# A decoder step on one Trainium2 core: the third sub-layer's conditioning moved from the opening stage into the first FFN

## The chip, the core and the metric

One core of a Trainium2 chip runs the whole kernel. TensorE (PE; its weight loads are listed as PEld), VectorE (DVE), ScalarE (ACT), GpSimd (POOL) and SyncE (SP, which here only issues transfers) each work through a queue of their own and wait for one another by semaphores. The metric is the time of one execution on the device, in microseconds (us).

## The reference

A decoder of two layers, each a token mixer and a SwiGLU feed-forward block (FFN), so four sub-layers. All activations are held transposed, 1024 features by 1056 tokens (1024 of the prompt, 32 of eight sampled sequences). Each sub-layer is conditioned: shift, scale and gate come from a product of the nine conditioning vectors with a 1024 x 3072 matrix.

```python
def modulation(c, w, b):
    m = jax.nn.silu(c) @ w + b
    shift, scale, gate = jnp.split(m, 3, axis=-1)
    return shift[:, None, :], scale[:, None, :], gate[:, None, :]

for i in range(DEPTH):
    sh, sc, gt = modulation(c, ada_w[i, 0], ada_b[i, 0])
    h = rmsnorm(x, norm_g[i, 0]) * (1 + sc) + sh
    ...                                   # layer 0: pooling mixer, layer 1: sparse attention
    x = x + gt * out
    sh, sc, gt = modulation(c, ada_w[i, 1], ada_b[i, 1])
    h = rmsnorm(x, norm_g[i, 1]) * (1 + sc) + sh
    x = x + gt * swiglu(h, ffn_w_in[i], ffn_w_out[i])
```

## The kernel before

Phases follow one another, with a barrier between them: `front_phase` (the opening stage: conditioning of sub-layers 1 to 3 and the pooling mixer), `ffn_phase` for layer 0, attention, `ffn_phase` for layer 1, the final norm.

**Conditioning.** The matrix of a sub-layer comes in six quads of 2 MB (QN = 6). For a quad, PE multiplies: 32 matmuls (64 records in the trace, since each fp32 matmul is recorded twice) whose stationary tile is 128 x 32, the nine vectors padded to 32, and which write four 32-row strips of bank 6 of PSUM (`multiply`, L337). ACT copies the sums to SBUF (L344), and PE turns them with one matmul into bank 7 (L352, two records). When all six quads are turned, DVE adds the bias and scales (L202, L205). `d.ada` lies in HBM as 24 quads, four sub-layers of six.

**Opening stage.** SP loads x and then the 18 quads of sub-layers 1 to 3 into a ring of three buffers (L437). After the first six quads come four pooling groups: DVE makes differences, ACT scales two tiles of the group (L459), PE multiplies them (L528), DVE adds the result to x (L562). The other twelve quads stand in PE's and ACT's queues between the groups, by the list `between`: quads 6 and 7 after group 0, 8 to 10 after group 1, 11 and 12 after group 2, 13 to 17 after group 3. After group 3 come also the products of the sampled tokens (L536) and their residual on DVE (L569, L570). The last steps of DVE are the conditioning of sub-layer 3.

**FFN.** It begins with an RMS norm: ACT squares (L247), PE sums over features (L255), DVE makes variance and reciprocal (L275, L280). The hidden size of 2816 is cut into N = 11 iterations. An iteration has three weight units of 1 MB: two hidden tiles of the up projection (each with a gate and an up side) and one unit of the down projection. Each fp32 unit is split into a high and a low part: ACT writes the high one (L677), POOL the rest (L718), and every product is three matmuls (L748 to L750, L768 to L770). Iteration 0 stands by itself; iterations 1 to 10 are a loop on each engine. In an iteration PE makes six groups of gate and up products (two tiles by three column chunks of 352 tokens; one group is 48 matmuls) and then, for each column chunk, eight down products (48 matmuls). SP loads the next iteration's units: unit 0 into `raw` 0 and unit 1 into `raw` 1 when POOL has split unit 2 of the current iteration, and unit 2 into `raw` 0 when it has split the next unit 0 (L662). Banks 0 to 5 of PSUM are in use; banks 6 and 7 are free after the norm.

The fourth sub-layer's conditioning is made during the attention's input stage, in half quads between fp32 matmuls (L369).

Of the kernel before, what the change touches and what calls it, by code (L numbers as in the profile page):

```python
# [14 lines left out]
ACT = mybir.ActivationFunctionType  # L15
# [8 lines left out]
P = 128  # L24
# [355 lines left out]
def front_phase(nc, c, d):  # L380
# [3 lines left out]
    with ExitStack() as ctx:  # L384
# [29 lines left out]
        block = ctx.enter_context(nc.Block())  # L414
        mod = QuadModulation(c, mrow, lambda n: ada[:, n % RING, :], lambda pe, n: pe.wait_ge(ada_ready[n % RING], 16 * (n // RING + 1)),
                             used, row_ready, turned, sums_read)
        NQ = (SUBS - 1) * QN

        between = [range(6, 8), range(8, 11), range(11, 13), range(13, NQ)]

        def cols(ch):
            return slice(ch * CH, (ch + 1) * CH)
# [118 lines left out]
        def _(dve):  # L541
# [77 lines left out]
            modulation(1)  # L619
            residuals(3)  # L620
            sample_residuals()
            modulation(2)
            dve.wait_ge(added, 24)


def ffn_phase(nc, c, d, layer):
# [3 lines left out]
    with ExitStack() as ctx:  # L630
# [12 lines left out]
        silu_ready, gated, a_step, a_ready = sem("silu_ready"), sem("gated"), sem("a_step"), sem("a_ready")  # L643
        added, rstep = sem("added"), sem("rstep")
        src = d.ffn[layer]
        block = ctx.enter_context(nc.Block())

        FIRST = [(a, ch) for ch in range(NCH) for a in range(2)]
# [2 lines left out]
        @block.sync  # L651
        def _(sp):

            sp.dma_start(raw[:, 0, :], src[0]).then_inc(raw_ready[0], 16)
            sp.dma_start(raw[:, 1, :], src[1]).then_inc(raw_ready[1], 16)
            sp.wait_ge(w_lo, 1)
            sp.dma_start(raw[:, 0, :], src[2]).then_inc(raw_ready[0], 16)
            with sp.Fori(0, N - 1) as i:
                for a in range(3):

                    sp.wait_ge(w_lo, i * 3 + (3, 2, 4)[a])
                    sp.dma_start(raw[:, a % 2, :], src[bass.ds(i * 3 + 3 + a, 1)].rearrange("a p n -> (a p) n")).then_inc(raw_ready[a % 2], 16)  # L662

        def raw_count(a, i):
            return (i * 16 + 16) if a == 1 else (i * 32 + (16 if a == 0 else 32))

        @block.scalar
        def _(act):
            def split_hi(a, i, first=False):
                act.wait_ge(raw_ready[a % 2], raw_count(a, i))  # L670
                if not first:

                    if a < 2:
                        act.wait_ge(up_ready, i * 6 - (3 if a == 0 else 0))
                    else:
                        act.wait_ge(down_ready, i * GD)
# [12 lines left out]
            norm.act_std(act, 1)  # L689
            split_hi(0, 0, True)  # L690
            norm.act_squares(act, 18, 24)
            norm.act_hi(act, 0, 8)
            split_hi(1, 0, True)
            norm.act_hi(act, 8, 14)
            silus(0, 1, 0)
            norm.act_hi(act, 14, 16)
            split_hi(2, 0, True)
            silus(1, 2, 0)
            norm.act_std(act, 2)
            norm.act_sample_hi(act)  # L700
            norm.act_hi(act, 16, 24)
            silus(2, 6, 0)
            act.wait_ge(up_ready, 6)
            for a in range(3):
                split_hi(a, 1)
            with act.Fori(1, N - 1) as i:
                silus(0, 3, i)
                split_hi(0, i + 1)
                silus(3, 6, i)
                split_hi(1, i + 1)  # L710
                split_hi(2, i + 1)
            silus(0, 6, N - 1)

        @block.gpsimd
# [12 lines left out]
        def _(pe):  # L727
            for ch in range(NCH):
                norm.pe_sums(pe, ch)

            def iteration(i, first):
                for n, (a, ch) in enumerate(FIRST if first else LATER):
                    pe.wait_ge(w_lo, 3 * i + (a + 1))
                    hi = whi[:, a, :].rearrange("p (k s m) -> p k s m", k=KD, s=2)
                    lo = wlo[:, a, :].rearrange("p (k s m) -> p k s m", k=KD, s=2)
                    col = slice(ch * CH, (ch + 1) * CH)
                    for side in range(2):
                        bank = 2 * (n % 3) + side
                        if n < 3 and not first:
                            pe.wait_ge(added, i * GD + (bank - 5))  # L740
                        if n >= 3:
                            pe.wait_ge(gated if side else silu_ready, i * 6 + (n - 2))
                        for k in range(KD):
                            if first and a == 0 and side == 0:
                                pe.wait_ge(norm.lo_ready, KD * ch + k + 1)
                                if ch == 2 and k == 0:
                                    pe.wait_ge(norm.s_lo, 1)
                            pe.matmul(c.ps[:, bank, 0:CH], hi[:, k, side, :], hhi[:, k, col], start=(k == 0), stop=False)  # L748
                            pe.matmul(c.ps[:, bank, 0:CH], lo[:, k, side, :], hhi[:, k, col], start=False, stop=False)  # L749
                            last = pe.matmul(c.ps[:, bank, 0:CH], hi[:, k, side, :], hlo[:, k, col], start=False, stop=(k == KD - 1))  # L750
                        last.then_inc(up_ready if side else gate_ready, 1)
                pe.wait_ge(w_lo, 3 * i + 3)
                hi = whi[:, 2, :].rearrange("p (k m) -> p k m", k=2)
                lo = wlo[:, 2, :].rearrange("p (k m) -> p k m", k=2)
                for ch in range(NCH):
                    col = slice(ch * CH, (ch + 1) * CH)
                    pe.wait_ge(a_ready, i * 6 + (2 * ch + 2 if first else NCH + ch + 1))
                    for m in range(KD):
                        q = ch * KD + m
                        if q < 6 and q % 2 == 0:  # L760
                            pe.wait_ge(silu_ready, i * 6 + (NCH + q // 2 + 1))
                        if q < 6 and q % 2 == 1:
                            pe.wait_ge(gated, i * 6 + (NCH + q // 2 + 1))
                        if q >= 6:
                            pe.wait_ge(added, i * GD + (q - 5))
                        w = slice(m * P, (m + 1) * P)
                        for k in range(2):
                            pe.matmul(c.ps[:, q % 6, 0:CH], hi[:, k, w], ahi[:, k, col], start=(k == 0), stop=False)  # L768
                            pe.matmul(c.ps[:, q % 6, 0:CH], lo[:, k, w], ahi[:, k, col], start=False, stop=False)  # L769
                            last = pe.matmul(c.ps[:, q % 6, 0:CH], hi[:, k, w], alo[:, k, col], start=False, stop=(k == 1))  # L770
                        last.then_inc(down_ready, 1)
            iteration(0, True)
            with pe.Fori(1, N) as i:
                iteration(i, False)

        @block.vector
        def _(dve):
# [49 lines left out]
            with dve.Fori(1, N) as i:  # L827
                for n, (a, ch) in enumerate(LATER):
                    gating(n, a, ch, i)
                residuals(i)  # L830
            dve.wait_ge(added, N * GD)


# [1381 lines left out]
```

## Time and profile before

| | |
|---|---|
| time, three runs | 2593.82, 2596.44, 2597.05 us; median 2596.44 |
| profiled execution | 2593.58 us, its span 2592.0 us |
| busy: PE, PEld | 2394.1 us (92%), 2061.1 us (80%) |
| busy: DVE, ACT, POOL | 1150.0, 670.6, 590.2 us |
| opening stage | 0 to 137 us |
| first FFN | 137 to 917 us |
| mean granted clock of PE | 0.969 of full speed |

The span is what the profiler saw of the execution on the core; the time contains it and 1.6 us around it. Busy time of an engine counts its instructions without register, branch, semaphore and transfer-issuing ones. A row of the timeline gives the start, the time to the end of the last of its merged instructions, engine, line, operation, tiles written and read with their shapes, the number of instructions, and in brackets the idle time of the engine before it and what ended it.

### The profile page before, as it was taken

The page shows a single profiled execution, that of the slowest core. Times are in us where ns is not written, and L with a number is a line of the kernel's source. Part 1 is how long each engine was busy: PE and PEld are TensorE (multiplying, and loading weights), DVE is VectorE, ACT ScalarE, POOL GpSimd, SP SyncE. Part 2 cuts the span into 40 slices and gives each one's busy share as a digit, 9 for nine tenths or more (in the row PEclk, how much of TensorE's full clock was granted, in tenths as well). Part 3 has the DMA queues.
Part 4 walks back from the last instruction along what each step waited for, and adds up shares of the span by engine and source line. Part 5 has one row for each costly group of instructions (what it writes and reads, how often), then busy time and mean ns, then how long its engine had stood idle before and what let it go on. Part 6 is the DMA issues. An engine that isn't in the chain of part 4 may idle for free. (4 is left out here: it accounts for less than half of the span.)

```text
span 2592.0 us, 39643 instructions
## 1 busy us (share of the span) xinstructions
PE 2394.1 (92%) x14980; PEld 2061.1 (80%) x14980; DVE 1150.0 (44%) x2604; ACT 670.6 (26%) x1193; POOL 590.2 (23%) x428
## 2 busy tenths in 40 slices
PE   4889999999999998899879976598999999999997
PEld 3679999999999964376535433397999999999995
DVE  7574333333333342787467631324633333333336
ACT  2151111111111042677167641204211111111101
POOL 2203112222122014200056643210221222221211
PEclk8999999999999999999989997799999999999998
DMA  9712111100111033243120019501101111111101
GB/s 403 296 51 82 49 49 49 49 29 36 49 49 49 0 139 106 85 144 115 56 84 17 9 55 308 210 18 50 61 38 49 49 49 49 49 49 49 49 0 67
DMA packets 67700, 206.59 MB, mean 80 GB/s; under 512 B 9589, under 2 KB 31637, under 8 KB 55061
## 3 DMA queue, kind: packets, MB, share of 16 engines
q1 hardware_dynamic: 54256, 179.01, 18.9%
q0 software_dynamic: 7920, 21.22, 2.5%
q10 hardware_dynamic: 5428, 5.12, 0.7%
q8 instruction: 57, 0.93, 0.1%
q14 instruction: 39, 0.31, 0.0%
HBM read 188.52 MB, written 16.13 MB: 79 GB/s over the span
## 5 line engine op out<-in xcount | busy, mean ns | idle before, releaser
L748 PE MATMUL ps<-f_hhi,f_whi 128*128 128x352 f32 x2112 | 682.6, 323 | 4.0 <-DVE f_hlo L295 3.6
L749 PE MATMUL ps<-f_hhi,f_wlo 128*128 128x352 f32 x2112 | 676.8, 320 | 0.0
L750 PE MATMUL ps<-f_hlo,f_whi 128*128 128x352 f32 x2112 | 676.5, 320 | 0.0
L718 POOL TENSOR_TENSOR f_wlo<-f_raw,f_whi 128x2048 fp32r<-128x2048 f32 x62 | 285.3, 4603 | 1224.7 <-ACT f_whi L677 1041.1
L80 DVE SCALAR_TENSOR_TENSOR xT<-ps,mod,xT 128x352 f32<-128x352 f32 (+1 forms) x552 | 313.9, 572 | 206.7 <-PE ps L770 121.6
L748 PEld LDWEIGHTS ps<-f_hhi,f_whi 128*128 128x128 f32 x2112 | 396.1, 188 | 8.2 <-DVE f_hlo L295 6.4
L749 PEld LDWEIGHTS ps<-f_hhi,f_wlo 128*128 128x128 f32 x2112 | 396.8, 188 | 0.0
L750 PEld LDWEIGHTS ps<-f_hlo,f_whi 128*128 128x128 f32 x2112 | 396.0, 188 | 0.0
L768 PE MATMUL ps<-f_ahi,f_whi 128*128 128x352 f32 x1056 | 340.6, 323 | 0.0
L769 PE MATMUL ps<-f_ahi,f_wlo 128*128 128x352 f32 x1056 | 338.4, 320 | 0.0
L770 PE MATMUL ps<-f_alo,f_whi 128*128 128x352 f32 x1056 | 338.2, 320 | 0.0
L677 ACT ACTIVATE f_whi<-f_raw 128x2048 fp32r<-128x2048 f32 x66 | 126.2, 1916 | 543.3 <-PE ps L770 414.9
L783 DVE TENSOR_TENSOR f1n_g<-f1n_sq,ps 128x352 f32<-128x352 f32 x66 | 34.4, 521 | 383.4 <-PE ps L750 382.7
L783 DVE TENSOR_TENSOR f0n_g<-f0n_sq,ps 128x352 f32<-128x352 f32 x66 | 34.4, 521 | 383.4 <-PE ps L750 382.6
L769 PEld LDWEIGHTS ps<-f_ahi,f_wlo 128*128 128x128 f32 x1056 | 198.4, 188 | 0.0
L768 PEld LDWEIGHTS ps<-f_ahi,f_whi 128*128 128x128 f32 x1056 | 198.1, 188 | 0.0
L770 PEld LDWEIGHTS ps<-f_alo,f_whi 128*128 128x128 f32 x1056 | 198.0, 187 | 0.0
L1647 POOL TENSOR_TENSOR pa_pr<-pa_pr,pa_rl 128x128 f32<-128x128 f32 (+7 forms) x128 | 143.9, 1146 | 162.3 <-DVE pa_rl L1635 162.2
L1086 PE MATMUL ps<-oT,ai_w 128*128 128x352 f32 x480 | 149.4, 466 | 0.0
L1625 DVE CUSTOM_DVE_ANT_0 pa_pr<-ps,mb 128x128 f32<-128x128 f32 (+7 forms) x128 | 91.9, 755 | 97.2 <-PE ps L1559 96.8
L1086 PEld LDWEIGHTS ps<-oT,ai_w 128*128 128x128 f32 x480 | 89.8, 191 | 48.3 <-issue 3.3
L684 ACT ACTIVATE f0n_sq<-ps 128x352 f32<-128x352 f32 x66 | 30.6, 465 | 340.2 <-PE ps L750 340.2
(311 smaller groups left out, 2832.7 us busy)
## 6 DMA issues: line engine op xcount, KB each, us to landing
f_raw<-in_ffn SPq DMA_DIRECT2D x66, 1024.0 KB, 4.8
ada_raw<-in_ada SPq DMA_DIRECT2D x18, 2048.0 KB, 12.3
sa_kv<-in_ckv POOLq DMA_DIRECT2D x54, 256.0 KB, 4.6
xT<-in_ada SPq DMA_DIRECT2D x12, 1024.0 KB, 5.4
sa_kv<-in_ckv SPq DMA_DIRECT2D x42, 256.0 KB, 4.7
ai_w<-in_win SPq DMA_DIRECT2D x6, 1024.0 KB, 7.1
xT<-in_ckv SPq DMA_DIRECT2D x23, 256.0 KB, 2.7
xT<-in_xT SPq DMA_DIRECT2D x8, 528.0 KB, 7.7
```

The lines of the kernel that those rows point to most:

```text
L80: ins = dve.scalar_tensor_tensor(out=x, in0=psum[:, 0:n], scalar=gate[:, 0:1], in1=x, op0=ALU.mult, op1=ALU.add)
L677: act.activation(whi[:, a, :], raw[:, a % 2, :], ACT.Copy).then_inc(w_hi, 1)
L718: pool.tensor_tensor(wlo[:, a, :], raw[:, a % 2, :], whi[:, a, :].bitcast(F32), ALU.subtract).then_inc(w_lo, 1)
L748: pe.matmul(c.ps[:, bank, 0:CH], hi[:, k, side, :], hhi[:, k, col], start=(k == 0), stop=False)
L749: pe.matmul(c.ps[:, bank, 0:CH], lo[:, k, side, :], hhi[:, k, col], start=False, stop=False)
L750: last = pe.matmul(c.ps[:, bank, 0:CH], hi[:, k, side, :], hlo[:, k, col], start=False, stop=(k == KD - 1))
L768: pe.matmul(c.ps[:, q % 6, 0:CH], hi[:, k, w], ahi[:, k, col], start=(k == 0), stop=False)
L769: pe.matmul(c.ps[:, q % 6, 0:CH], lo[:, k, w], ahi[:, k, col], start=False, stop=False)
L770: last = pe.matmul(c.ps[:, q % 6, 0:CH], hi[:, k, w], alo[:, k, col], start=False, stop=(k == 1))
L1086: ins = pe.matmul(c.ps[:, n % 4, 0:CH], wt[:, k, job[1] * P:(job[1] + 1) * P], h[:, k, cols(job[2])], start=(k == 0), stop=(k == KD - 1))
L1625: dve.tensor_tensor_reduce(out=probs(i, 2 * sp + a, 0, L), in0=src, in1=c.mb[:, MB0[q]:MB0[q] + L], scale=-SCALE, scalar=-NEG, op0=ALU.add ...
L1647: pool.tensor_tensor(p, p, rl[:, s // 2 % 4, r:r + 1].to_broadcast([P, (pairs[i][0] + 1) * P]), ALU.mult).then_inc(p_ready, 1)
```

## The change

The opening stage makes twelve quads instead of 18: 6 and 7 after group 0, 8 and 9 after group 1, 10 and 11 after group 2, none after group 3; the third sub-layer's two DVE steps go with it. In the first FFN each of iterations 1 to 6 makes one quad of the third sub-layer, in four parts of 16 matmul records on PE: after the second and the sixth up group and after the first and second chunk of the down products. After the third chunk PE turns the quad. The weights come in quarter quads of 512 KB, in pieces of 1 KB, into the norm's `rstd` buffer, which is free by then; a part's load waits until the part before is used. ACT copies the sums between the splits of units 1 and 2. DVE makes the two steps of the conditioning after the last residual of the FFN. The FFN's loops on SP, ACT and PE are cut in two: iterations 1 to 6 with the new work, 7 to 10 without. The second FFN gets none.

```diff
-        NQ = (SUBS - 1) * QN
-        between = [range(6, 8), range(8, 11), range(11, 13), range(13, NQ)]
+        NQ = 2 * QN
+        between = [range(6, 8), range(8, 10), range(10, NQ), []]
...
             sample_residuals()
-            modulation(2)
...
+        PARTS = 4
+        COND = QN if layer == 0 else 0
+        ada = norm.rstd[:, 0:2 * UNIT // PARTS].rearrange("p (j k m) -> p j k m", j=4, k=KD // PARTS)
...
+                with sp.Fori(1, COND + 1) as i:
+                    load(i, (0, 1))
+                    for part in range(PARTS):
+                        if part == 1:
+                            load(i, (2,))
+                        sp.wait_ge(mod_used, i * PARTS + (part + 1 - PARTS))
+                        quad = d.ada[bass.ds(i + (2 * QN - 1), 1)].rearrange("a p (j k m) -> (a p) j k m", j=4, k=KD)
+                        sp.dma_start(ada, quad[:, :, KD // PARTS * part:KD // PARTS * (part + 1), :]).then_inc(ada_ready, 16)
...
                 split_hi(1, i + 1)
+                if conditioning:
+                    act.wait_ge(mod_used, i * PARTS + 1)
+                    act.wait_ge(turned, i)
+                    act.activation(mrow[:, :], c.ps[:, 6, 0:P], ACT.Copy).then_inc(row_ready, 1)
                 split_hi(2, i + 1)
...
+            def condition(i, part):
+                pe.wait_ge(ada_ready, i * (16 * PARTS) + 16 * (part + 1 - PARTS))
+                if part == 0:
+                    pe.wait_ge(row_ready, i)
+                for k in range(KD // PARTS):
+                    for j in range(4):
+                        last = pe.matmul(c.ps[32 * j:32 * j + 32, 6, 0:P], c.silu[:, KD // PARTS * part + k, :], ada[:, j, k, :],
+                                         start=(part == 0 and k == 0), stop=(part == PARTS - 1 and k == KD // PARTS - 1))
+                last.then_inc(mod_used, 1)
+            def turn(i):
+                pe.wait_ge(row_ready, i + 1)
...
+                pe.matmul(out, mrow[:, :], pick, start=True, stop=True).then_inc(turned, 1)
...
+                    if conditioning and n in (1, 5):
+                        condition(i, n // 5)
...
+                    if conditioning and ch < 2:
+                        condition(i, 2 + ch)
+                    if conditioning and ch == 2:
+                        turn(i)
...
                 residuals(i)
+            if COND:
...
+                Modulation(c, None, None, None, None, None, turned, sums_read).apply(dve, 2, QN + 1, 0, link)
             dve.wait_ge(added, N * GD)
```

## Rows read from the trace of the kernel before

**Rows 1.** The page, part 1: span and busy time of PE and its weight loads.

```profile
span 2592.0 us, 39643 instructions
PE 2394.1 (92%) x14980; PEld 2061.1 (80%) x14980; DVE 1150.0 (44%) x2604; ACT 670.6 (26%) x1193; POOL 590.2 (23%) x428
```

**Rows 2.** By stretches: length, busy us (instructions) per engine, granted clock, DMA share, GB/s.

```profile
65.00:130.00 65.00, 52.88 (x834) 40.16 (x832) 36.55 (x56) 9.27 (x17) 13.32 (x15) 0.97 0.78 295
260.00:325.00 65.00, 65.00 (x411) 65.00 (x410) 24.23 (x58) 8.11 (x9) 11.07 (x3) 1.00 0.13 49
```

**Rows 3.** Timeline, end of the opening stage and start of the FFN.

```profile
116.31 1.95 PE L337 MATMUL ps<-ada_raw,silu 128*32 128x128 f32 x64
116.88 0.42 DVE L570 TENSOR_TENSOR xT<-xT,pool_tmp 128x256 f32<-128x256 f32 x1
119.00 1.95 PE L337 MATMUL ps<-ada_raw,silu 128*32 128x128 f32 x64
136.11 0.38 DVE L202 TENSOR_TENSOR mod<-ps,vec 128x216 f32<-128x216 f32 x1 [18.80 <-PE ps L352]
136.52 0.23 DVE L205 SCALAR_TENSOR_TENSOR mod<-mod,vec 128x72 f32<-128x72 f32 x1
137.28 2.04 ACT L247 ACTIVATE f0n_sq<-xT 128x352 f32<-128x352 f32 x5 [1.74 <-PEq L384]
```

**Rows 4.** Timeline, from quad 10 to the pooling group behind it.

```profile
89.31 2.18 ACT L459 ACTIVATE pool_df<-pool_df,mod 128x1024 f32<-128x1024 f32 x2
91.54 7.15 PE L528 MATMUL ps<-pool_df,pool_raw 128*128 128x352 f32 x24 [1.66 <-ACT pool_df L459]
```

**Rows 5.** The FFN's start: two stretches (as rows 2), then two rows of the timeline.

```profile
140.00:142.00 2.00, 2.00 (x5) 1.23 (x4) 0.00 (x0) 0.65 (x3) 0.00 (x0) 0.50 1.00 414
152.00:154.00 2.00, 0.81 (x3) 0.59 (x4) 1.97 (x2) 2.00 (x5) 0.00 (x0) 1.00 0.00 0
...
137.82 7.88 PE L255 MATMUL ps<-f0n_sq,ones 128*128 128x352 f32 x20 [1.82 <-ACT f0n_sq L247]
144.56 0.52 DVE L275 TENSOR_SCALAR f0n_rstd<-ps 128x352 f32<-128x352 f32 x1 [7.80 <-PE ps L255]
```

**Rows 6.** Timeline of PE, attention's input stage: half quads between wide fp32 matmuls.

```profile
979.81 27.38 PE L1069 MATMUL ps<-oT,ai_w 128*128 128x352 f32 x92
...
1089.80 0.28 PE L1128 MATMUL ps<-ai_part,rowsum 128*128 128x1 f32 x2
1090.00 1.08 PE L369 MATMUL ps<-xT,silu 128*32 128x128 f32 x32
1091.01 3.23 PE L1086 MATMUL ps<-oT,ai_w 128*128 128x352 f32 x10
1094.08 0.28 PE L1128 MATMUL ps<-ai_part,rowsum 128*128 128x1 f32 x2
1094.22 0.39 PE L352 MATMUL ps<-ident,ai_mrow 128*128 128x36 f32 x2
1094.54 1.08 PE L369 MATMUL ps<-xT,silu 128*32 128x128 f32 x32
```

**Rows 7.** Page, part 5 (mean ns); L337 alone (ns min/median/max); timeline at a switch of width.

```profile
L770 PE MATMUL ps<-f_alo,f_whi 128*128 128x352 f32 x1056 | 338.2, 320 | 0.0
...
L337 PE MATMUL ps<-ada_raw,silu x1152: 272/273/423, 22.1 to 134.8; 128*32 128x128 f32 x192
...
98.62 1.69 PEld L337 LDWEIGHTS ps<-ada_raw,silu 128*32 128x32 f32 x64 [0.44 <-issue]
```

**Rows 8.** An FFN iteration's weight units: timeline, one stretch, loads (us to landing).

```profile
298.26 1.92 ACT L677 ACTIVATE f_whi<-f_raw 128x2048 fp32r<-128x2048 f32 x1 [20.91 <-PE ps L770]
305.03 0.92 SPq L662 DMA_DIRECT2D f_raw<-in_ffn  x2
...
311.00:312.00 1.00, 1.00 (x8) 1.00 (x7) 0.00 (x0) 0.00 (x0) 0.00 (x0) 1.00 0.57 238
...
f_raw<-in_ffn SPq DMA_DIRECT2D x66, 1024.0 KB, 4.8
```

More of the change, by code:

```diff
@@ L645, in ffn_phase @@
         src = d.ffn[layer]
+        PARTS = 4
+        COND = QN if layer == 0 else 0
+        ada = norm.rstd[:, 0:2 * UNIT // PARTS].rearrange("p (j k m) -> p j k m", j=4, k=KD // PARTS)
+        mrow = sb("mrow", [P, P]) if COND else None
+        ada_ready, mod_used, row_ready, turned, sums_read, m_step = [sem(n) for n in ("ada_ready", "mod_used", "row_ready", "turned", "sums_read", "m_step")]
         block = ctx.enter_context(nc.Block())
@@ L657, in _, with load @@
             sp.dma_start(raw[:, 0, :], src[2]).then_inc(raw_ready[0], 16)
-            with sp.Fori(0, N - 1) as i:
-                for a in range(3):
+            def load(i, units):
+                for a in units:
                     sp.wait_ge(w_lo, i * 3 + (3, 2, 4)[a])
                     sp.dma_start(raw[:, a % 2, :], src[bass.ds(i * 3 + 3 + a, 1)].rearrange("a p n -> (a p) n")).then_inc(raw_ready[a % 2], 16)
+            with sp.Fori(0, 1) as i:
+                load(i, (0, 1, 2))
+            if COND:
+                sp.wait_ge(norm.lo_ready, KD * NCH)
+                sp.wait_ge(norm.s_lo, 1)
+                with sp.Fori(1, COND + 1) as i:
[6 more added lines that the diff above has]
+                        sp.dma_start(ada, quad[:, :, KD // PARTS * part:KD // PARTS * (part + 1), :]).then_inc(ada_ready, 16)
+            with sp.Fori(COND + 1, N - 1) as i:
+                load(i, (0, 1, 2))
         def raw_count(a, i):
@@ L705, in _, with body @@
                 split_hi(a, 1)
-            with act.Fori(1, N - 1) as i:
+            def body(i, conditioning):
                 silus(0, 3, i)
@@ L710, in _ @@
                 split_hi(1, i + 1)
+                if conditioning:
+                    act.wait_ge(mod_used, i * PARTS + 1)
+                    act.wait_ge(turned, i)
+                    act.activation(mrow[:, :], c.ps[:, 6, 0:P], ACT.Copy).then_inc(row_ready, 1)
                 split_hi(2, i + 1)
+            if COND:
+                with act.Fori(1, COND + 1) as i:
+                    body(i, True)
+            with act.Fori(COND + 1, N - 1) as i:
+                body(i, False)
             silus(0, 6, N - 1)
@@ L729, in _, with iteration @@
                 norm.pe_sums(pe, ch)
-            def iteration(i, first):
+            def condition(i, part):
[9 more added lines that the diff above has]
+                pe.wait_ge(row_ready, i + 1)
+                pick = c.ident[:, :].rearrange("p (j e) -> p j e", j=4)[:, :, 0:NSQ]
+                out = c.ps[:, 7, bass.ds(i * (4 * NSQ) - 4 * NSQ, 4 * NSQ)].rearrange("p (j e) -> p j e", j=4)
+                pe.matmul(out, mrow[:, :], pick, start=True, stop=True).then_inc(turned, 1)
+            def iteration(i, first, conditioning=False):
                 for n, (a, ch) in enumerate(FIRST if first else LATER):
@@ L771, in iteration @@
                         last.then_inc(down_ready, 1)
+                    if conditioning and ch < 2:
+                        condition(i, 2 + ch)
+                    if conditioning and ch == 2:
+                        turn(i)
             iteration(0, True)
-            with pe.Fori(1, N) as i:
+            if COND:
+                for counter in (mod_used, row_ready, turned):
+                    pe.sem_inc(counter, 1)
+                with pe.Fori(1, COND + 1) as i:
+                    iteration(i, False, True)
+            with pe.Fori(COND + 1, N) as i:
                 iteration(i, False)
@@ L830, in _, with link @@
                 residuals(i)
+            if COND:
+                steps = [0]
+                def link(ins):
+                    steps[0] += 1
+                    ins.then_inc(m_step, 1)
+                    dve.wait_ge(m_step, steps[0])
+                Modulation(c, None, None, None, None, None, turned, sums_read).apply(dve, 2, QN + 1, 0, link)
             dve.wait_ge(added, N * GD)
```

## The prediction

> **What bounds the kernel now.** I read the page's busy shares first: TensorE (PE) works 92% of the span [rows 1]. That is a mean over stages, so the table by stretches comes next, and it shows two stages of different kind. In the first feed-forward block (FFN) PE and its weight loads are busy without a gap: 411 matmuls in 65.00 us, one each 0.158 us, at the full granted clock, while no other engine fills half its time [rows 2]. Whatever PE is given there lengthens the kernel by its full duration. In the opening stage (65 to 130 us) PE works 53 of 65 us [rows 2]; there the order of the work decides, and the timeline shows it. Third view: what PE does last in the opening stage. From the sample residuals (VectorE, DVE, done at 116.88 + 0.42 = 117.30 us) to the first square of the FFN (ScalarE, ACT, 137.28 us) nothing happens but the last five quads of the third sub-layer's conditioning and its two DVE steps [rows 3]. So the change takes work from a place where it alone is on the path and puts it where PE is full. The question is only the price in each.
>
> **What is removed.** (a) Five quads and the conditioning's two DVE steps after the fourth pooling group: from 117.30 to 136.52 + 0.23 = 136.75 us, 19.45 us [rows 3]. (b) One quad fewer ahead of the fourth group: quad 10 now follows group 2 and quad 12 is gone. A quad costs 119.00 - 116.31 = 2.69 us there, because product, ACT copy and turn follow one another [rows 3]. It is on the path: ACT scales the next group's tiles (89.31 us) only behind the copy of the last quad's sums, which stands ahead in its queue, and PE's pooling matmuls wait for that scaling (91.54) [rows 4]. Sum: 22.1 us. Late next would be the DVE residuals; they follow the same PE chain and move with it. The weight queue on SP is empty then, so the FFN's first loads start as soon as before. No piece of it stays: bound from 19.5 (b gains nothing) to 22.1; I take 22.1, since the chain in rows 4 is complete.
>
> (c) The clock at the FFN's start. Before, PE came from the last quads, short bursts between waits for weights and copies, and between 140 and 142 us it had 0.50 of its clock, so the first twenty records of the sums took 7.88 us [rows 5]. Between 152 and 154 us, after a wait that followed solid work, it kept 1.00 [rows 5]. With the change PE comes from solid pooling matmuls and a wait of about 2 us. The first chunk's sixteen records then take 16 x 0.296 = 4.7 us (27.38 us for 92 such records [rows 6]); with 0.3 for the last one's end the variance on DVE could start at 137.82 + 5.0 = 142.8 instead of 144.56 [rows 5]: 1.7 us, on the path, since square root and every later tile follow it. Bounds 0 and 1.7; I take 1.7, the case nearest to the row at 152.
>
> **What is added on PE.** In each of iterations 1 to 6: 64 narrow matmul records (32 output columns) in four parts of 16, and one turn of two records. Nothing hides them. Streaming: 64 records take 1.95 us, the last one's own 0.27 apart, so 0.0267 us each; a part streams 0.43 us. But each part stands among wide matmuls. The trace has this for the fourth sub-layer, half a quad between fp32 matmuls of the attention input [rows 6]: 32 records occupy 1091.01 - 1090.00 = 1.01 us where streaming gives 0.85 (0.16 on leaving); the ten wide records behind them need 1094.08 - 1091.01 = 3.07 where ten of 0.296 are 2.96 (0.11, a weight load not hidden); entering costs 0.20 (1089.80 to 1090.00) against 0.14 where no narrow block follows (1094.08 to 1094.22), 0.06. So 0.33 us for each insertion, whatever its size, and a part costs 0.43 + 0.33 = 0.76. The turn takes 1094.54 - 1094.22 = 0.32, with the entry into a narrow block; 0.26 without. Per iteration 4 x 0.76 + 0.26 = 3.30 us, six times: 19.8 us. Splitting a quad in four thus costs more PE time (3.3) than the serial quad did in the opening stage (2.69). Bounds of a part: 0.43, if the neighbours cover the switch, and 0.98, if the whole pause of 0.44 us in the weight loads that stands at such a switch in the opening stage [rows 7] comes on top of the streaming and of the 0.11 behind it. I take 0.76, from the row with the same narrow tiles between dense wide ones.
>
> [...]
>
> What a full drain would do, from rows: a wide FFN record lasts 0.32 and follows at 0.158, so entering costs 0.16; a narrow one lasts 0.27 and follows at 0.107 for four, so leaving costs 0.17; with the 0.11 a part costs 0.87, the six iterations 22.4 us [rows 2, 7].
>
> **What is added elsewhere.** ACT: one copy an iteration, which waits for the fourth part. Queued behind it is the split of the third unit, and that waits for the end of the down products anyway, 7.6 us (48 x 0.158) later. PE's turn waits for that copy with the same 7.6 us in hand. Cost 0. DVE: the two steps (0.38 + 0.23, 0.65 with the gap [rows 3]) now follow the FFN's last residual, and the phase ends with them: +0.7.
>
> SP: four loads of 0.5 MB an iteration. Parts 1 to 3 have time: a part's buffer is free when the part before is used, 7.6 us or more ahead of its use, and a load twice as big lands in 4.8 us [rows 8]. The load of unit 2 is queued behind part 0 only, which waits for nothing. **Part 0 is tight.** Its load is queued on SP behind units 0 and 1 of the next iteration, which start when GpSimd has split unit 2: 298.26 (end of the down products) to 305.03 [rows 8]. Their data flow until the slice 311 to 312, 57% of it [rows 8]; half a megabyte more at that rate ends near 312.9, with 1 KB pieces and the receipt 313.4 to 313.8. PE wants it after two column blocks, 96 x 0.158 = 15.2 us after 298.26, plus the turn: 313.5 to 313.7. So PE waits 0 to 0.4 us in each iteration; I take 0.2, 1.2 us in all. Bounds 0 and 6 (1 us in each).
>
> **The sum.** -22.1 - 1.7 + 19.8 + 1.2 + 0.7 = -2.1 us. The profiled execution took 2593.58 us (span 2592.0), 2.9 under the median of the three runs, 2596.44; the sum is made in its rows and applied to the median: 2594.3 us.
>
> **Rivals.**
> 1. *The switches are covered.* FFN matmuls take half the time of the fp32 ones in rows 6, so what surrounds a part is not the same; if they hide the switch, a part costs near 0.43, six iterations 11.9, and the kernel gains 10.0: 2586. From 0.63 a part it is faster by over 5.2 us. For it: PE's gaps at group ends in the FFN are nil [rows 2]. Against it: rows 6.
> 2. *Part 0 comes late* (the other side). PE is stopped behind a wait in every conditioning iteration, by the queue of 2 MB ahead of it. If it lands 1.4 us after PE wants it, 8.4 us instead of 1.2, and with the clock's 1.7 not won: +6.8, 2603. It decides from some 1.2 us per iteration on. For it: there is no margin in the rows 8. Against it: the data rate leaves 0.4 at most.
> 3. *Full drain*, as priced above: +0.5, 2597, which no measurement here tells from the forecast.
> 4. *The opening stage doesn't shorten as said*, because another end takes over (the pooling tail's output, GpSimd's wait for it): half the gain lost would give +9, 2605. That output follows DVE's tail step, which moves earlier too, so little speaks for it.
>
> **How the numbers follow.** Forecast 0.42, full drain 0.15, covered switches 0.25, late part 0 0.15, opening not shortened 0.03. About 0.2%, 5.2 us, can be told from no change; forecast and drain lie inside: same 0.57, faster 0.25, slower 0.18. The range takes a part at 0.58 with no wait (-22.1 - 1.7 + 15.5 + 0.7 = -7.6) and a part at 0.9 with the clock not won and 0.4 us of waiting (-22.1 + 23.2 + 2.4 + 0.7 = +4.2): 2588.8 to 2600.6, widened to 2588.5 and 2601.5 for a piece of rival 2. The far ends of rivals 1 and 2 stay out.
>
> **What the changed profile would show.** The FFN's first square near 115 us instead of 137.28; sums matmuls at clock 1.00 behind it; iterations 1 to 6 of 68.7 + 3.3 + 0.2 us, 7 to 10 unchanged at 68.7 (432 x 0.159); at a part, 16 narrow records within 0.43 and the next wide record about 0.3 later than streaming alone; no PE idle released by the weight load at parts 1 to 3, some tenths at part 0; the DVE steps 0.7 us behind the last residual. A wait of a microsecond at part 0, an iteration under 71.2 or over 73.4 us, or an FFN start later than 118 us would make the forecast wrong.

## The result, and the profile after

The changed kernel takes 2597.79 us (median of 20 runs, 2593.14 to 2602.45); the kernel before, in the runs beside it, 2593.51. The ratio is 1.0017 with a 95% interval of 1.0010 to 1.0024: 4.4 us more, between 2.6 and 6.2. The forecast was 2.1 us less. The profiled execution of the changed kernel took 2601.43 us. Its page, part 1, against [rows 1]:

```profile
span 2599.8 us, 39755 instructions
PE 2406.2 (93%) x14980; PEld 2064.0 (79%) x14980; DVE 1151.0 (44%) x2604; ACT 671.1 (26%) x1193; POOL 591.3 (23%) x428
```

PE has the same number of matmul records and is busy 12 us longer. The end of the opening stage, against [rows 3] and [rows 4] (timeline: start, length, engine, line, operation):

```profile
102.02 2.17 ACT L459 ACTIVATE pool_df<-pool_df,mod 128x1024 f32<-128x1024 f32 x2
...
104.25 8.85 PE L528 MATMUL ps<-pool_df,pool_raw 128*128 128x352 f32 x24 [1.66 <-ACT pool_df L459]
112.93 4.19 PE L536 MATMUL ps<-pool_fs,pool_raw 128*128 128x32 f32 x32
...
117.61 0.42 DVE L570 TENSOR_TENSOR xT<-xT,pool_tmp 128x256 f32<-128x256 f32 x1
118.55 1.65 ACT L247 ACTIVATE f0n_sq<-xT 128x352 f32<-128x352 f32 x4 [14.36 <-PEq L384]
```

The first square follows the sample residual after 0.94 us and not after 20.40. It stands at 118.55 and not near 115: pooling group 3, at half clock from 105.6 to 109.0, took 8.85 us where group 2 took 7.15 [rows 4], the products of the samples took 4.19 us and not 3.65, and DVE's first conditioning step came 1.6 us later than in the first profile of the kernel before. (Half clock is a granted clock of 0.50.) The next view is the table by stretches (length, busy us (instructions) of PE, PEld, DVE, ACT, POOL, granted clock, DMA share, GB/s), against [rows 2] and [rows 5]: the opening stage, the first sums, iterations 1, 3 and 7.

```profile
65.00:130.00 65.00, 55.30 (x543) 39.08 (x542) 41.14 (x61) 15.92 (x30) 14.82 (x16) 0.92 0.36 134
119.00:122.00 3.00, 2.90 (x5) 1.85 (x6) 0.00 (x0) 1.85 (x6) 0.00 (x0) 0.50 0.83 268
211.10:284.89 73.79, 72.05 (x500) 70.31 (x499) 24.47 (x59) 8.82 (x10) 13.81 (x3) 1.00 0.21 72
357.39:429.41 72.02, 72.02 (x502) 70.36 (x500) 24.37 (x59) 8.82 (x10) 13.82 (x3) 1.00 0.21 73
646.39:715.13 68.74, 68.74 (x436) 68.74 (x434) 24.10 (x58) 8.55 (x9) 13.83 (x3) 1.00 0.13 47
```

The first sums run at half clock again. Iteration 3 takes 3.3 us more than iteration 7; iteration 1 takes 73.79 us, with PE idle for 1.7 of them. The timeline of a part of 16 records, with the wide matmuls around it (against [rows 6]), and of the turn:

```profile
259.33 0.32 PE L801 MATMUL ps<-f_hlo,f_whi 128*128 128x352 f32 x1
259.59 0.64 PE L772 MATMUL ps<-f0n_rstd,silu 128*32 128x128 f32 x16
260.16 0.43 PE L821 MATMUL ps<-f_ahi,f_whi 128*128 128x352 f32 x1
260.43 0.32 PE L822 MATMUL ps<-f_ahi,f_wlo 128*128 128x352 f32 x1
...
429.11 0.32 PE L823 MATMUL ps<-f_alo,f_whi 128*128 128x352 f32 x1
429.27 0.30 PE L780 MATMUL ps<-ident,f_mrow 128*128 128x36 f32 x2
429.41 0.41 PE L799 MATMUL ps<-f_hhi,f_whi 128*128 128x352 f32 x1
429.65 0.32 PE L800 MATMUL ps<-f_hhi,f_wlo 128*128 128x352 f32 x1
```

From 259.33 to 260.43 there are 1.10 us; without the part there would be two spacings of 0.159, so the part costs 0.78. The turn: 429.65 - 429.11 - 2 x 0.159 = 0.22. The last lines are for part 0 of iteration 1, against [rows 8]: SP's issues, and PE's wait for the load.

```profile
218.14 0.98 SPq L669 DMA_DIRECT2D f_raw<-in_ffn  x2
219.41 0.70 SPq L683 DMA_DIRECT2D f0n_rstd<-in_ada  x1
...
226.24 0.32 PE L801 MATMUL ps<-f_hlo,f_whi 128*128 128x352 f32 x1
228.30 0.64 PE L772 MATMUL ps<-f0n_rstd,silu 128*32 128x128 f32 x16 [1.74 <-DMA f0n_rstd<-in_ada]
```

One profile of each kernel doesn't settle a difference of 4 us, since the stretches at half clock lie elsewhere from profile to profile (pooling group 3 takes 8.85 us in the first of the changed kernel and 7.15 in the second). So both were profiled again (experiment 6), and the stages, read from the timelines, stand beside the terms of the prediction (us):

| stage | before (3 profiles) | changed (2 profiles) | predicted | measured |
|---|---|---|---|---|
| start to DVE's first conditioning step | 53.84, 55.51, 55.30 | 55.41, 55.27 | 0 | +0.5 |
| to the last sample residual (L570) | 63.04, 63.01, 62.77 | 62.20, 60.19 | -2.7 | -1.7 |
| to the FFN's first square | 20.40, 20.56, 20.54 | 0.94, 0.95 | -19.45 | -19.6 |
| to the first up matmul | 19.53, 19.53, 19.53 | 19.60, 20.81 | -1.7 | +0.7 |
| iteration 0 | 72.60, 72.94, 72.45 | 72.94, 72.45 | 0 | 0 |
| iterations 1 to 6 | 411.96, 412.01, 411.96 | 435.29, 434.63 | +21.0 | +23.0 |
| to the attention's first square | 277.28, 277.30, 277.30 | 278.04, 278.06 | +0.7 | +0.8 |
| sum | | | -2.1 | +3.6 |

The sum by stages, 3.6, lies in the runs' interval of 2.6 to 6.2. It is not the whole difference between these profiles: their spans are 2592.0, 2590.6 and 2589.9 us before and 2599.8 and 2600.0 after, 9.1 apart in the mean, so 5.5 us lie behind the attention's first square, where the code is the same. That stretch takes 1667.2 to 1673.3 us in the seven profiles of this case without quads in the FFN and 1672.8 to 1678.7 in the seven with them. The runs leave room for at most some 3 us of it; whether any of it is an effect of the change stays open.

### The profile page after: what moved, and what is told of

It is laid out like the page before. It is cut to its first block and busy times, and to the rows that moved or that the text cites. A ratio compares the mean times of both kernels' runs of the same rounds, so it can differ in the third digit from the quotient of the medians.

```text
span 2599.8 us, 39755 instructions
## 1 busy us (share of the span) xinstructions
PE 2406.2 (93%) x14980; PEld 2064.0 (79%) x14980; DVE 1151.0 (44%) x2604; ACT 671.1 (26%) x1193; POOL 591.3 (23%) x428
## 3 DMA queue, kind: packets, MB, share of 16 engines
q1 hardware_dynamic: 66064, 179.01, 19.2%
```

## The experiments

**1. Only the removal.** The third sub-layer's conditioning isn't made at all.

```diff
-        COND = QN if layer == 0 else 0
+        COND = 0
...
             modulation(1)
+            link(dve.tensor_copy(c.mod[:, 2], c.mod[:, 1]))
```

> Only the removal: the opening without the third sub-layer's six quads, and nothing in the FFN in their place. The third sub-layer's conditioning is left out of the computation (it takes the second's vectors, one copy on VectorE), so the time is that of the cheaper opening alone. Theory A, the prediction's term: the opening gives 22.1 us, and the total is 21 to 23 us under the kernel before (about 2571.5 beside 2593.5). Theory A with the clock term of the prediction: 23.8 us under. Theory B, read from the one profile of the changed kernel, whose first square came 18.7 us earlier: the opening gives 18 to 19 us, because the stretches at half clock in the opening last as long as before.

Measured: ratio to the kernel before 0.9912 (0.9895 to 0.9929), 22.8 us less, between 18.4 and 27.2. The middle lies between theory A's 22.1 and its 23.8 with the clock term; the interval excludes neither, and of theory B's 18 to 19 only the lower end.

**2. Only the addition.** All eighteen quads stay in the opening stage (`NQ` and `between` as before, `modulation(2)` kept), and the FFN makes six of them again.

> Only the addition: the opening as before, with all eighteen quads and the third sub-layer's conditioning made there, and the six quads made a second time in iterations 1 to 6 of the first FFN, as in the change. The prediction's terms: 19.8 us on TensorE, 1.2 us for the weights of part 0 and 0.7 us on VectorE, so 21.7 us over the kernel before. Theory A, with the sizes in the profile of the changed kernel: 20.1 us for parts and turns, 2.4 us for part 0's waits, 0.8 us by which the matmuls behind part 0 follow each other more slowly, 0.7 us on VectorE: 24 us over. Theory B, that the addition costs as predicted and the opening gave less: 21 to 22 us over.

Measured: 1.0106 (1.0083 to 1.0129), 27.5 us more, between 21.5 and 33.5. The total holds both theories, but the two halves add up to +4.7, near the change's own +4.4, so no further mechanism is needed; with the intervals of both halves this sum is known to some 7 us only. In its profile iterations 1 to 6 take 436.24 us, 24.3 more than before, and part 0 of iteration 1 waits again, 2.0 us. Some 1.5 of the 24.3 are a stretch at half clock right behind that wait (253.6 to 257.0 us); in the two profiles of the changed kernel no such stretch follows it.

**3. Part 0's load ahead of the units.**

```diff
                 with sp.Fori(1, COND + 1) as i:
-                    load(i, (0, 1))
                     for part in range(PARTS):
                         if part == 1:
-                            load(i, (2,))
+                            load(i, (0, 1, 2))
```

> The changed kernel with one line of SyncE moved: part 0 is asked for ahead of units 0 and 1 of the iteration, and no longer behind the wait for unit 1's buffer. If TensorE's waits for the quarter quad at part 0 (2.1 us and 0.4 us in the profile of the changed kernel) come from the place of that issue in the queue, the total falls by 2.0 to 2.8 us against the changed kernel (about 2595.3 beside 2597.8). If they come from the free buffer, or from how long the transfer takes, it falls by under 0.5 us; if unit 0 or 1 comes late in its stead, it rises.

Measured: 1.0004 (0.9995 to 1.0013) where the changed kernel has 1.0017, 3.4 us less by the ratios, and by their intervals between 0.4 and 6.3. Its profile (issues on SP, PE at part 0, stretches of iterations 1 and 2, and the times from issue to landing of the 24 loads, least, median, most; the last line is the changed kernel's):

```profile
206.75 0.70 SPq L682 DMA_DIRECT2D f0n_rstd<-in_ada  x1
216.39 0.97 SPq L669 DMA_DIRECT2D f_raw<-in_ffn  x2
...
224.69 0.64 PE L771 MATMUL ps<-f0n_rstd,silu 128*32 128x128 f32 x16
...
209.34:281.29 71.95, 71.95 (x501) 70.29 (x499) 24.53 (x60) 8.83 (x10) 13.82 (x3) 1.00 0.23 78
281.29:353.31 72.02, 72.02 (x502) 70.36 (x500) 24.41 (x59) 8.82 (x10) 13.82 (x3) 1.00 0.21 73
...
DMA to landing us min/median/max: 3.6/3.7/6.0
```

```profile
DMA to landing us min/median/max: 3.6/4.9/8.8
```

The load is issued 18 us ahead of its use and not 7, PE has no idle time in the two iterations, and units 0 and 1 aren't late. Iterations 1 to 6 take 432.07 us: the queue ahead of part 0 cost 3.2 and 2.6 us in the two profiles of the changed kernel, and 20.1 us are left for parts and turns. Some 0.8 of the 3.2 was not a wait: behind part 0 of iterations 2 and 6 the wide matmuls followed at 0.161 us where 0.159 is usual. Here, and in the second profile of the changed kernel, it is absent or half as large; its cause stays open.

**4. Two insertions instead of four.** The same 64 records an iteration, in two blocks of 32 behind the sixth up group and the second down chunk; the second quarter's weights lie in free parts of other buffers.

```diff
-                    if conditioning and n in (1, 5):
-                        condition(i, n // 5)
+                    if conditioning and n == 5:
+                        condition(i, 0)
...
-                    if conditioning and ch < 2:
-                        condition(i, 2 + ch)
+                    if conditioning and ch == 1:
+                        condition(i, 1)
```

> The changed kernel with the same matmuls in two insertions of 32 for an iteration and not in four of 16, behind the sixth up group and the second down group, with a second buffer for the weights. Theory A, an insertion has a price of its own, about 0.35 us beside the time of its matmuls: 12 insertions fewer give 4.2 us; the first insertion no longer waits for its weights (2.4 us), and the up groups behind the second one keep the spacing that they had (0.8 us): 6 to 7.5 us under the changed kernel, near 2591 beside 2597.8, which is 2 to 3 us under the kernel before. Theory B, the price goes with the matmuls and not with the insertions: only the waits are saved, 2 to 3 us under the changed kernel. Theory C, longer insertions let VectorE or the weight units fall behind: no gain.

Measured: 0.9998 (0.9990 to 1.0007), 4.9 us under the changed kernel (by the intervals 2.1 to 7.8), level with the kernel before. Iterations 1 and 2 in its profile, and a block of 32:

```profile
208.26:279.49 71.23, 71.23 (x501) 70.40 (x499) 24.54 (x60) 8.82 (x10) 13.81 (x3) 1.00 0.22 75
279.49:350.79 71.30, 71.30 (x502) 70.47 (x500) 24.42 (x59) 8.82 (x10) 13.82 (x3) 1.00 0.21 74
...
253.87 0.32 PE L813 MATMUL ps<-f_hlo,f_whi 128*128 128x352 f32 x1
254.13 0.64 PE L784 MATMUL ps<-f0n_rstd,silu 128*32 128x128 f32 x16
254.59 0.40 PE L784 MATMUL ps<-f0n_sq,silu 128*32 128x128 f32 x8
254.81 0.40 PE L784 MATMUL ps<-f_rest,silu 128*32 128x128 f32 x8
255.14 0.43 PE L833 MATMUL ps<-f_ahi,f_whi 128*128 128x352 f32 x1
255.41 0.32 PE L834 MATMUL ps<-f_ahi,f_wlo 128*128 128x352 f32 x1
```

The block costs 255.41 - 253.87 - 2 x 0.159 = 1.22 us, a part of 16 costs 0.78. So 16 records stream in 0.44, and an insertion has a price of its own, 0.34 us with 16 records and with 32: theory A, and the prediction's 0.43 and 0.33. Iterations 1 to 6 take 427.75 us, 6.9 and 7.5 less than in the two profiles of the changed kernel, as A says; the runs show 4.9, and their interval alone would hold theory B's 3 too, so A rests on the two blocks in the trace. The difference of some 2 us between profile and runs isn't explained.

The full drain of the prediction, in which at a change of width each record waits for the end of the one ahead, was its author's estimate, priced from rows at 0.87 for a part; the measured 0.78 is 0.09 less. In these two traces the next record starts 0.06 or 0.07 us before the recorded end of the one ahead: entering a part or block at 259.59 beside 259.33 + 0.32 and at 254.13 beside 253.87 + 0.32, leaving it at 260.16 beside 259.59 + 0.64 and at 255.14 beside 254.81 + 0.40. Among wide records it is 0.16 (0.32 long, 0.159 apart).

**5. The pause ahead of the FFN filled.**

```diff
                 quads(between[g])
+            pe.wait_ge(sums_read, 2)
+            for _ in range(3):
+                pe.matmul(c.ps[:, 7, 0:CH], w[:, 3, 0, 0:P], df[:, 7, 0:CH], start=True, stop=True)
```

> The changed kernel with three 128 x 352 matmuls of no use on TensorE behind the sample tokens' last matmul, in the 2 us in which it waits for the first FFN's first square. The prediction took 1.7 us off for the clock at the start of the FFN, since the pause ahead of it is gone; in the profile of the changed kernel the granted clock is at half from 115.9 to 122.7 us all the same, and the way from the first square to the first up matmul is 19.6 us. Theory A, the pause of 2 us that is left lowers the clock: with the fillers no half-clock stretch touches the FFN's first sums, and the way is 17.9 us, as in the second FFN of the kernel before. Theory B, the pause is not it (the 32 matmuls of 128 x 32 ahead of it, or what went before): a stretch of half clock is there still, and the way is 19.5 us or more.

Measured, one profile (table by stretches, the first sums and a later stretch of the norm):

```profile
119.00:122.00 3.00, 2.97 (x10) 2.01 (x11) 0.00 (x0) 2.81 (x7) 0.00 (x0) 1.00 0.82 279
133.00:135.50 2.50, 2.50 (x5) 1.50 (x5) 2.50 (x2) 1.35 (x5) 0.00 (x0) 0.50 0.00 0
```

Neither theory: the first sums run at full clock, but a stretch at half clock comes later in the same stage, and the way from the first square to the first up matmul is 19.2 us, not 17.9. The fillers also delay the first square by 0.7 us. From the sample residual to the first up matmul it is 20.9 us, beside 20.5 to 21.8 in the kernels without fillers. In this profile closing the pause moved the loss and didn't remove it; one profile is a sign, not a proof.

Where the half clock went says more. It falls on the third chunk's sums, the same place as the row at 152 us of the kernel before, which kept 1.00 [rows 5]. What PE did just before is the same in both: the second chunk's wide sums and a wait of 2.15 us (first this kernel, then the kernel before):

```profile
125.56 5.00 PE L255 MATMUL ps<-f0n_sq,ones 128*128 128x352 f32 x16 [0.35 <-ACT f0n_sq L247]
132.71 5.42 PE L255 MATMUL ps<-f0n_sq,ones 128*128 128x352 f32 x12 [2.15 <-ACT f0n_sq L247]
...
146.05 5.00 PE L255 MATMUL ps<-f0n_sq,ones 128*128 128x352 f32 x16 [0.35 <-ACT f0n_sq L247]
153.19 3.82 PE L255 MATMUL ps<-f0n_sq,ones 128*128 128x352 f32 x12 [2.15 <-ACT f0n_sq L247]
```

So the same work just ahead is followed by either clock, and no narrow matmul stands directly ahead of this half-clock stretch.

**6. Both kernels again.** (The expectations speak of thirteen quads; the changed opening stage has twelve.)

> The kernel before, once more, for a second profile of its opening. In the first one the first conditioning step on VectorE came at 53.84 us, ahead of all the kernels with the same code up to there (54.95, 55.41, 55.67 and 55.80; one at 53.76), and the first up matmul at 156.81 us. Theory A, the opening of before takes some 157 to 158 us as a rule, and the change's opening gives less than the 22.1 us of the sum (19 to 20 us in the mean of four profiles without the five quads): the first up matmul is at 156 to 158 us. Theory B, that profile was a lucky one, and the term is right: 158 to 161 us.

> The kernel before, a third profile of its opening, with the same question: theory A puts the first up matmul at 156 to 158 us, theory B at 158 to 161 us; the mean of the three decides, beside 138.2, 138.0, 136.9 and 135.8 us in the four kernels whose opening has thirteen quads.

> The changed kernel, a second profile. Theory A: iterations 1 to 6 take again 23 to 24 us more than in the kernel before, 20.2 us of it parts and turns, and TensorE waits again about 2 us for part 0 of iteration 1. Theory B, the waits and the wider spacing of the matmuls behind part 0 belong to the one execution: 20 to 21.5 us more. The way from the first square to the first up matmul is 19.5 us or more again if the clock term is not to be had, 17.9 us if its loss was chance.

Measured: the first up matmul of the kernel before is at 158.61 and 158.15 us, with the first profile's 156.80 in the mean 157.9. In the kernels with twelve quads and no fillers (the changed one twice, experiments 1, 3 and 4) it is at 138.2, 137.2, 138.0, 136.9 and 135.8, in the mean 137.2. So the opening stage and the norm give 20.6 us and not the predicted 23.8; the 157.9 lies at the border between the two theories, and the gain lies between A's 19 to 20 and B's 22.1, nearer to A's. The changed kernel again has the wait, and its first sums again stand at half clock (PE at part 0; a stretch as above):

```profile
226.57 0.65 PE L772 MATMUL ps<-f0n_rstd,silu 128*32 128x128 f32 x16 [1.48 <-DMA f0n_rstd<-in_ada]
...
119.00:122.00 3.00, 3.00 (x7) 1.75 (x6) 0.00 (x0) 1.02 (x3) 0.00 (x0) 0.50 1.02 426
```

Iterations 1 to 6 take 22.7 us more, a little under theory A's 23 to 24, well over B's 21.5.

**7. The quads in the gaps.** Is the opening stage a dear place, or only its end? In the kernel before, with nothing moved to the FFN; DVE's conditioning steps of the second and third sub-layer move up with their quads:

```diff
-        between = [range(6, 8), range(8, 11), range(11, 13), range(13, NQ)]
+        between = [range(6, 10), range(10, 14), range(14, NQ), []]
...
             residuals(1)
+            modulation(1)
...
-            modulation(1)
+            modulation(2)
             residuals(3)
             sample_residuals()
-            modulation(2)
```

> The kernel before with its eighteen quads in the opening, but with the last twelve in the three gaps between the groups, four in each, and none behind the last group; VectorE makes the second and third sub-layers' conditioning one and two places earlier. Nothing is added to the FFN. Theory A, the five quads cost 19.5 us because of where they stand (behind everything, one after the other through TensorE, ScalarE and the load of the next, with VectorE's step behind the last): in a gap a quad costs 2.70 us, as between two groups in the profile of the kernel before, so 5 more in the gaps cost 13.5 us, and the fourth of a gap waits 0 to 1 us for its weights, as only three buffers are there: 3 to 6 us under the kernel before. Theory B, the weights' transfers set the pace wherever the quads stand (the last two of the five wait 2.5 and 2.1 us for them in a profile of the kernel before): the fourth quad of each gap comes 3 us or more late, and the time is within 2 us of the kernel before, or over it.

Measured: 1.0025 (1.0013 to 1.0037), 6.5 us more. The 19.5 us behind the last group are gone (0.95 us are left), but the fourth quad of each gap waits for its weights. Its three waits, in the timeline:

```profile
75.57 1.95 PE L337 MATMUL ps<-ada_raw,silu 128*32 128x128 f32 x64 [1.75 <-DMA ada_raw<-in_ada]
99.88 1.95 PE L337 MATMUL ps<-ada_raw,silu 128*32 128x128 f32 x64 [2.97 <-DMA ada_raw<-in_ada]
124.66 3.21 PE L337 MATMUL ps<-ada_raw,silu 128*32 128x128 f32 x64 [3.43 <-DMA ada_raw<-in_ada]
```

8.15 us of waits: theory B. Two of the three pooling groups behind them are in part at half clock (8.85 us where 7.15 is usual), and one in the first profile of before. With three buffers a gap held three quads without waiting here, not four.

**8. ScalarE's order.** In the same kernel, the scaling of the next group's tiles ahead of the copies of the gap's quads:

```diff
-            for g in range(4):
-                for j in (2 * g, 2 * g + 1):
+            for g in range(5):
+                for j in (2 * g, 2 * g + 1) if g < 4 else ():
...
-                for n in between[g]:
+                for n in between[g - 1] if g else ():
```

> The same, and on ScalarE the scaling of the next group's two rows stands ahead of the copies of the gap's quads and not behind them. If the 1.66 us of TensorE's idle time ahead of each of groups 1 to 3 is the wait for that scaling alone, three times 1.66 us go: 4 to 5 us under the same kernel without it. If VectorE's differences or residuals come late in its stead, or the first quad's copy waits behind the scaling (2.2 us), less than half of it is left.

Measured: 1.0010 (0.9999 to 1.0021), 3.9 us under the one without it by the ratios; the intervals hold 4 to 5 and also nothing. In its profile group 1 follows the last quad's turn after 0.25 us (81.77 to 82.02) where it was 2.08 in experiment 7 (77.92 to 80.00). The way was then tried on the kernel of experiment 4 and on the kernel before:

> The kernel with the two insertions of 32, and on ScalarE the scaling of the next group's two rows ahead of the copies of the gap's quads. With at most three quads in a gap no quad waits for its weights there, so if the 1.66 us of TensorE's idle time ahead of each of groups 1 to 3 goes (it did where four quads stood in a gap), 4 to 5 us go: 2587 to 2590 us where the same kernel without it took 2593.5, under both kernels of the case. If VectorE's differences of rows 6 and 7 or its residuals are late instead, under 2 us.

> The kernel before with the same exchange on ScalarE and nothing else, so that what the exchange gives and what the two insertions give can be told apart: three times 1.66 us, 4 to 5 us under the kernel before, if its gaps shorten as they do in the other kernel. Theory B: with eighteen quads the loads of the weights set the pace from the first gap on, what the gaps give comes back as waits of the five last quads for their weights, and it stays within 2 us of the kernel before. In that case the move into the FFN and this exchange need one another.

Measured: 0.9966 (0.9954 to 0.9978) with the two insertions, 2585.56 us, 8.8 us under the kernel before; 0.9972 (0.9961 to 0.9983) on the kernel before, 7.3 us under it (4.4 to 10.1). Both beat both kernels of the case. Both gain more than the 4 to 5 us expected, though their intervals still reach down to it: the first is 8.3 under the same kernel without the exchange. The 1.5 us between the two can't be told from nothing. PE ahead of groups 1 to 3 with the two insertions, and, last, the waits for weights among the five last quads on the kernel before:

```profile
72.00 7.12 PE L528 MATMUL ps<-pool_df,pool_raw 128*128 128x352 f32 x24 [0.82 <-DVE xT L562]
...
84.35 7.13 PE L528 MATMUL ps<-pool_df,pool_raw 128*128 128x352 f32 x24
...
94.64 0.41 PE L352 MATMUL ps<-ident,ada_mrow 128*128 128x36 f32 x2 [1.28 <-ACT ada_mrow L344]
...
122.07 1.95 PE L337 MATMUL ps<-ada_raw,silu 128*32 128x128 f32 x64 [2.43 <-DMA ada_raw<-in_ada]
126.95 3.20 PE L337 MATMUL ps<-ada_raw,silu 128*32 128x128 f32 x64 [2.12 <-DMA ada_raw<-in_ada]
```

The 1.66 us ahead of each group [rows 4] are gone; 0.82 and 0.88 (1.28 - 0.40) come back as waits for DVE, directly or through ACT. Theory B of the last expectation falls: the five last quads wait 2.43 and 2.12 us for their weights, as they did without the exchange (2.48 and 2.10). On the kernel before, the way from DVE's first conditioning step to the first up matmul is 98.3 us in one profile, beside 103.0 in the mean of three without the exchange: 4.7 less, within the runs' interval; what the runs show beyond it isn't explained. So most of this gain comes from ACT's order, not from the place of the third sub-layer's quads: at its best, with two insertions, that move was worth about what it cost, to within some 4 us.

## Why the prediction was wrong, step by step

The shape was right: PE full in the FFN, the opening stage's end empty, a gain of about 20 against a cost of about 20. By the stages the forecast was 5.7 us off on a difference of two such numbers (by the runs 6.5). Three of the signs that it named against itself appeared: the first square at 118.55 us (at 116.40 in the second profile, within what it allowed), a wait of 1.7 and 1.5 us at part 0, and iteration 1 at 73.79 and 73.87 us. The measured change lies inside the stated range, near the end that was built from the clock not won and waits at part 0, and those two came. By the terms:

- **(a) The end of the opening stage**, 19.45 us: right (19.6).
- **(b) One quad fewer ahead of group 3**, 2.69 us: the chain is right. From group 1's scaling to group 2's the third profile of before takes 16.89 us and the changed kernel 14.20, both at full clock, 2.69 apart. But over the stage 1.7 is what arrives: the changed kernel's two profiles need 62.20 and 60.19 us, since in the first of them group 3 and the sample products ran in part at half clock. Experiments 3 and 4 have such a stretch there too (15.06 us from group 3's scaling to L570), experiment 1 and the second profile don't (13.37).
- **(c) The clock at the FFN's start**, -1.7: **the step that failed**, worth 2.2 to 2.4 us. The prediction counted on full clock in the first sums, since PE comes "from solid pooling matmuls" and one row, at 152 us, had kept 1.00 after solid work. They stand at half clock in all five profiles of this start without fillers, and also in those of the three kernels of experiments 7 and 8 that start the FFN the same way. In the five, the way to the first up matmul is 19.53 to 20.88 us, in the mean 0.5 more than before. The size was right where the clock is full: in experiment 5 the variance on DVE starts 5.03 us after the first sum (119.03 to 124.06), as worked out. What was wrong is the row as a rule: experiment 5 shows half clock at that very place behind the same work. The prediction also overlooked that 32 matmuls of 32 columns (L536) stand between the pooling matmuls and the pause, though the description of the kernel names them. Why the clock falls stays open: in the first profile half clock is granted from 115.9 us on, while they run, in the second from 116.2 on, in the pause; what share the narrow matmuls have was not tried. Of its two bounds, 0 was the better one, and a loss should have been left in.
- **Parts and turns on PE**, 19.8: right (20.1), and experiment 4 confirms the two pieces, 0.43 for streaming and 0.33 for an insertion. Covered switches and full drain are out.
- **Part 0's weights**, 1.2: mis-sized, 2.6 to 3.2. The step that failed there is the claim that one row stands for all six iterations. In iterations 2 to 6 the load is at the edge, as worked out (0 to 0.4 us). The 0.5 to 0.9 us that the prediction adds for the pieces and the receipt are its author's estimate; in the profile of before the second unit's data end at 311.6 us (DMA share 0.97 from 311.4 to 311.6, then 0.02), and the load, issued at 305.6, lands 6.6 us later, at 312.2. In iteration 1 part 0's load is issued 8.3 us after the iteration's start and lands 8.8 us later (8.5 in the second profile), and PE waits 1.7 and 1.5 us; in iterations 2 to 6 it is issued 8.1 us after the start and lands 7.3 to 7.7 us later, behind the same 2 MB. Why the first one is slower stays open. It is the second rival's mechanism, in one iteration and not in all, at a third of its price, joined to its other condition, the clock not won.
- **DVE's two steps**, 0.7: right (0.7 to 0.8). ACT, POOL and SP for parts 1 to 3 cost nothing, as said: the only waits on a load in iterations 1 to 6 are at part 0.

Added up: 1.0 (b) + 2.4 (c) + 0.3 (parts) + 1.7 (part 0) + 0.5 ahead of DVE's first conditioning step, where the code is the same, less 0.2 in small terms: 5.7 us.

## What to carry to other kernels

Here work moved onto the full TensorE paid its streaming time (0.44 us for 16 records) plus 0.34 us for each insertion, and two insertions of 32 were cheaper than four of 16: count the insertions, and make them as few as buffers allow. A small load queued behind big ones has to be checked in every iteration (here it was late above all in the first, in all three profiles with that queue: PE waited 1.7, 1.5 and 2.0 us). Before work is moved out of a chain, look at why the chain is long: here one engine's queue held the next group's scaling behind copies for a later stage, and exchanging them gave 7 to 8 us where the move, at its best, gave nothing that can be told from zero. When two terms of 20 us nearly cancel, a clock term of 1.7 us can decide the sign, and one row isn't enough for it: the same place has to be looked at in several executions, or both signs belong in the sum.

## What the runs showed of the hardware

- The same code met the half clock at other places in other profiles. In the kernel before, pooling group 1 takes 8.85, 8.85 and 7.15 us in the three profiles; the granted clock in it is 0.50 from 74.2 to 77.4 us in the first and 1.00 from 76.0 to 82.0 in the third. In the changed kernel group 3 takes 8.85 and 7.15 us.
- Half clock (0.50) was granted in the sums at the FFN's start in all eight profiles in which the 128 x 32 matmuls and a pause of 1.98 to 1.99 us come directly before them; their first twenty records take 7.77 to 9.23 us, beside 6.18 at full clock in experiment 5. There, with three wide matmuls in the pause, it came some 15 us later in the same stage (one profile).
- A quarter-quad load of half a megabyte took 3.6 us at the least in the changed kernel, and 7.3 to 8.8 us where it is queued behind two of 1 MB.
